# A transformer block in fp32 accuracy on one core: the last moving tile of each change is loaded and split at another place

## The reference

```
u = _rms(h, g_mlp_pre[l])
f = jnp.square(jax.nn.relu(u @ w_ff1[l])) @ w_ff2[l]
h = h + _rms(f, g_mlp_post[l])
```

## Time and profile before

| | |
|---|---|
| median of 3 runs | 2652.94 us (2649.47 to 2654.08) |
| profiled execution, span | 2651.5 us (its own time isn't given beside the span) |
| PE busy | 2577.2 us, 97% |
| DVE, ACT, POOL busy | 1621.5, 1212.6, 334.6 us |
| TensorE's mean granted clock | 0.990 |

### The profile page before, as it was taken

How to read it: one execution, slowest core, us unless ns; L and a number is a source line. 1 busy time by engine, 2 the same in 40 slices (tenths; PEclk the granted TensorE clock), 3 DMA queues, 4 the chain that set the end, 5 groups by cost and what they waited for, 6 DMA issues and landing times.

```text
span 2651.5 us, 35377 instructions
## 1 busy us (share of the span) xinstructions
PE 2577.2 (97%) x12220; PEld 2118.7 (80%) x12220; DVE 1621.5 (61%) x3488; ACT 1212.6 (46%) x2177; POOL 334.6 (13%) x366
## 2 busy tenths in 40 slices
PE   8999999999998999999999999999999999999998
PEld 8998787666676888877877888878887887878786
DVE  6223304989995766764468777766757465564665
ACT  6112312676774555654445333533335343443554
POOL 2110001222221221220000000000000001111133
PEclk9999999899999999999999999999999999999999
DMA  7323457543533111126667667757655365666787
GB/s 235 124 102 117 120 160 243 137 101 80 126 127 92 29 46 40 29 68 189 187 227 224 214 216 230 225 158 231 195 153 177 107 222 104 164 164 158 184 173 139
DMA packets 331516, 398.85 MB, mean 150 GB/s; under 512 B 23488, under 2 KB 237744, under 8 KB 323024
## 3 DMA queue, kind: packets, MB, share of 16 engines
q1 hardware_dynamic: 313776, 364.68, 44.0%
q0 software_dynamic: 17568, 31.99, 8.4%
HBM read 240.13 MB, written 156.48 MB: 150 GB/s over the span
## 4 chain that ended last, share of the span: by engine, by line
PE 61%; DVE 3%; ACT 2%; DMA 1%; issue 1%; SPq 1%; POOL 0%; DVEq 0%; ACTq 0%; POOLq 0%
PE ff_ps_x L3163 25%; PE ff_ps_m L3163 13%; PE ff_ps_z L3163 6%; PE ml_ps_s L2042 6%; PE ff_ps_m L1602 4%; PE ml_ps_o L2071 4%; PE ml_ps_t L2055 2%; DMA ml_v_raw<-scr_yT 1%; DVE ff_mv_lo_p L3014 1%; DMA ff_pieces<-scr_acc 0%; PE ff_ps_r L2602 0%; PE mo_ps_t L2619 0%; ACT ff_mv_hi_p L2896 0%; SPq L2229 0%; DVE ff_pieces L2332 0%
## 5 line engine op out<-in xcount | busy, mean ns | idle before, releaser
L3163 PE MATMUL ff_ps_x<-ff_mv_hi_p,ff_st_hi_p 128*128 128x512 f32 x764 | 299.0, 391 | 12.0 <-DVE ff_mv_lo_p L3014 11.4
L3163 PE MATMUL ff_ps_x<-ff_mv_hi_p,ff_st_lo_p 128*128 128x512 f32 x764 | 298.6, 391 | 0.0
L3163 PE MATMUL ff_ps_x<-ff_mv_lo_p,ff_st_hi_p 128*128 128x512 f32 x764 | 298.3, 390 | 0.0
L2042 PE MATMUL ml_ps_s<-wide,ml_qs 128*128 128x416 f32 (+14 forms) x880 | 196.5, 357 | 3.2 <-PEq L137 2.7
L3009 DVE TENSOR_TENSOR ff_st_lo_p<-ff_ps_m,ff_st_hi_p 128x512 fp32r<-128x512 f32 x190 | 130.8, 689 | 103.7 <-ACT ff_st_hi_p L2886 103.7
L2853 POOL DMA_DIRECT2D scr_acc<-ff_pieces x64 | 55.4, 872 | 1026.2 <-DVE ff_pieces L3033 947.0
L3163 PEld LDWEIGHTS ff_ps_x<-ff_mv_hi_p,ff_st_hi_p 128*128 128x128 f32 x764 | 144.0, 188 | 44.2 <-issue 13.6
L2903 ACT ACTIVATE ff_u<-ff_ps_x 128x512 f32<-128x512 f32 x128 | 76.6, 599 | 214.4 <-PE ff_ps_x L3163 214.4
L3163 PEld LDWEIGHTS ff_ps_x<-ff_mv_hi_p,ff_st_lo_p 128*128 128x128 f32 x764 | 144.0, 188 | 30.2
L3163 PEld LDWEIGHTS ff_ps_x<-ff_mv_lo_p,ff_st_hi_p 128*128 128x128 f32 x764 | 144.1, 189 | 29.9
L2042 PEld LDWEIGHTS ml_ps_s<-wide,ml_qs 128*128 128x128 f32 x880 | 151.0, 191 | 19.1 <-issue 7.0
(11 more groups left out here) (300 smaller groups left out, 6383.3 us busy)
## 6 DMA issues: line engine op xcount, KB each, us to landing
st_raw<-in_w_ff SPq DMA_DIRECT2D x64, 512.0 KB, 6.2
scr_hid<-ff_pieces SPq DMA_DIRECT2D x128, 256.0 KB, 2.6
st_raw<-scr_hid SPq DMA_DIRECT2D x64, 512.0 KB, 5.1
ring<-in_w_ff SPq DMA_DIRECT2D x28, 1024.0 KB, 7.9
scr_t<-ring SPq DMA_DIRECT2D x24, 1024.0 KB, 6.4
ring<-scr_t SPq DMA_DIRECT2D x21, 1024.0 KB, 8.3
scr_acc<-ff_pieces POOLq DMA_DIRECT2D x64, 256.0 KB, 4.1
ring<-scr_u SPq DMA_DIRECT2D x13, 1024.0 KB, 8.3
```

The lines of the kernel that those rows point to most:

```text
L2042: m = pe.matmul(ps_s[n % NSB][:, 0:w], q, k, start=j == 0, stop=j == len(pairs) - 1)
L3163: m = pe.matmul(bank[:, :], w[kind][:, k], a[kind][:, k], start=start and k == 0 and i == 0, stop=stop and k == KH - 1 and i == 2, skip_gr ...
```

## The change

Three orders are altered, and no instruction is added or taken away. SyncE issues the load of the `p4` tile in front of `load_raw(n+2)` at the first step of a group. ScalarE makes its high half before the split of `p2`, VectorE its low half before the sum `c11` and the split of `p2`.

```diff
             def quarters(n):
-                if starts(n):
-                    load_moving(group_of(n), "p4")
                 if ends(n):
...
                 if n:
                     store("c21", n - 1)
-                if n >= 0 and n + 2 <= LAST:
+                if starts(n):
+                    load_moving(group_of(n), "p4")
+                if n + 2 <= LAST:
                     load_raw(n + 2)
                 quarters(n)
...
             for n in range(PLAIN + 1, LAST + 1):
+                if starts(n):
+                    load_moving(group_of(n), "p4")
                 if n + 2 <= LAST:
                     load_raw(n + 2)
...
# ScalarE
-                then("p2", n)
                 if starts(n):
                     moving("p4", group_of(n))
+                then("p2", n)
...
# VectorE
                     mean(n - 1, 0, 2)
+                if starts(n):
+                    moving("p4", group_of(n))
                 if n:
                     dve.wait_ge(product_done, done("p2", n))
                     add("c11", n, ps_z, s1, c11_made)
                 then("p2", n)
                 hidden("c11", n, c11_made)
-                if starts(n):
-                    moving("p4", group_of(n))
```

## The result

| | median | range, runs |
|---|---|---|
| before | 2652.94 us | 2649.47 to 2654.08, 5 |
| changed | 2636.0 us | 2634.19 to 2637.34, 5 |

The kernel before has two more runs here than in its first table; the median stayed. The medians differ by 16.9 us; 2638.0 us was forecast. The ratio of the runs is 0.9943, 95% interval 0.9931 to 0.9955, which is 15.1 us less (11.9 to 18.3). The span of the profiled execution fell from 2651.5 to 2635.5 us (2636.5 forecast).

The account below looks back on a forecast made before the run. TensorE, busy 97% of the span, was taken to bound the kernel. 15.95 - 5 x 0.2 = 14.95 us off the 2651.5 us span gave 2636.5, plus 1.4 for the median: 2638.0 us, range 2634.5 to 2643.0.

Parts of the forecast that it names:

- the cost of a change: TensorE at five moving-tile changes: 11.4 us of gaps plus 4.55 us of slow products behind them, together 15.95 us.
- ScalarE's and VectorE's splits: Step 16: ScalarE's tile copy begins at 1723.93 instead of 1726.27, VectorE's low half runs 1725.86 to 1728.16.
- The residue: Left at each change on TensorE: 0.1 us lateness plus up to 0.12 us slower first matmuls; 0.2 us taken.
- The load: SyncE issues the p4 tile 1.3 us earlier in step 16; landing 0.7 us before ScalarE comes, at old flight.
- rival B: Tile lands no earlier or VectorE's order costs: ScalarE waits 0.6 us each change, 3.2 us in all; 2641.2 us; chance 0.09.
- rival A: Clock still falls at two changes, steps 40 and 56, though gaps go: 3.46 us stay, 2641.4 us; chance 0.11.
- C: VectorE's 1.8 us of lead were needed each change; TensorE waits for a later low half, 9 us back, 2647 us; chance 0.04.
- D: Tile lands late, holding up both splits: at five changes 15.4 us more than before, 2668 us; chance 0.03.
- E: Reorder moves nothing because ScalarE doesn't come to the p4 tile earlier: 2653 us; chance 0.05.

Follow-up runs that it names:

- splits alone: Changed kernel with SyncE's old order, so the p4 load stays behind the raw rows: 2636.18 us against 2649.96 us before, ratio 0.9945.
- one product earlier: Changed kernel with ScalarE's p4 split also ahead of the p7 copy, VectorE's ahead of sum c22: 2633.31 us against 2649.96 us before, ratio 0.9932.
- VectorE's order kept: Changed kernel with VectorE's low half of p4 back behind sum c11 and the split of p2: 2642.37 us against 2649.96 us before, ratio 0.9968.
- load alone: Kernel before with only SyncE's p4 load moved ahead of the raw rows, both splits in old order: 2651.41 us against 2649.96 us, ratio 0.9999.
- ScalarE's order kept: Changed kernel with ScalarE's split of p4 back behind that of p2: 2650.51 us against 2651.91 us before, ratio 0.9999.
- double copy: Kernel before with ScalarE's copy of the p4 tile made twice at the five changes: 2663.83 us against 2651.91 us, ratio 1.0047.
- late tile: Changed kernel with the p4 load behind the raw rows and a wait for p3's next low half: 2665.51 us against 2651.91 us before, ratio 1.0054.

## Why the prediction was right

- **What bounds the kernel, and the cost of a change** (15.95 us): right. The clean length of the feed-forward fell by 14.9 us, for 14.95 us forecast.
- **ScalarE's and VectorE's splits:** right to 0.1 us in each place. The two experiments that move only one of them show that both were needed.
- **The residue** (0.2 us taken, 0.1 to 0.24 bounded): measured 0.21 to 0.24, at the upper end. The product behind was to take about 2.8 us; counted from the end of `p1` it takes 2.93 to 2.96. It goes to zero once the low half is ready earlier, so it was the 0.1 us of lateness and what a restart costs besides.
- **The load:** right in kind, too cautious in size, and of little weight. The flight with nothing large ahead was 5.2 to 7.2 us instead of the 7.6 to 9.1 us used. The margins at steps 32 and 56 on which rival B rested, worked out as 0.3 and 0.2 us, were 3.1 and 2.3 us, and with the old order of SyncE only 0.8 us would have been lost.
- **The falls of the clock** (rival A): they belong to the gaps. The products behind the gaps, read from the chain of waits of ten profiles:

| gap on TensorE | kernels | changes | with a fall of the clock | slow product of 2.72 us takes |
|---|---|---|---|---|
| none or up to 0.4 us | changed, splits alone, one product earlier | 15 | 0 | 2.72 to 3.00 |
| 1.1 to 1.7 us | VectorE's order kept | 5 | 0 | 2.96 to 3.00 |
| 2.3 us | before (twice), load alone, ScalarE's order kept | 20 | 8 | 4.2 to 4.6 |
| 4.1 us | double copy | 5 | 5 | 4.5 to 5.5 |
| 3.8 to 5.5 us | late tile | 5 | 5 | 4.3 to 5.5 |

  What the Trainium skill says (TensorE: Matmul & The Clock Gate, section "Why this matters for your kernels"), that long gaps between bursts cost the clock, holds here; what would follow from its figure, that gaps of this length are safe, doesn't: at 2.3 us 8 of 20 had a fall. The measurement decides, and the two falls were rightly put into the sum. Away from the gaps there are none: in stretches of 6 us from 1418 to 2600 us the granted clock of the changed kernel is 1.00 throughout, and so it is with VectorE's order kept and with both splits one product earlier. The price of the two falls, 3.46 us, is a little too high, since the 1.85 us of step 56 hold the 0.28 us of a restart at full clock: 3.2 us is left, and with VectorE's order kept 3.3 us came back. The sum of 15.95 us doesn't change by it, only rival A's time.
- **The time.** 2 us below the point. The feed-forward explains none of it, since it gained 14.9 us for 14.95. The rest is within what executions of one kernel differ by: the five runs of before lie within 4.6 us, those of the changed kernel within 3.2 us, and the profiles enter the feed-forward anywhere within 6.1 us. So it is partly luck that the medians came within 2 us; the length of the feed-forward is what bears the sum out.
- **Rivals C, D and E:** C's cover held. In the changed kernel VectorE, behind the late sum, stands idle again for 0.89 us from about 1732.6 us and for 2.03 us from about 1734.2, so not all of its lead was used up; how much later it could run isn't shown. D's mechanism is real and cost 16.8 us in the profiled execution, but needs this tile to land more than 3 us later than it did in the changed kernel. E is excluded by ScalarE's timeline.

## What to carry to other kernels

Where an engine works through an order written by hand, look at what an instruction waits for *by its place*: a long tile copy whose own data were ready stood behind a short one that waited for the last product, and 2.3 us of TensorE's time a change hung on that alone. Move the whole chain (load, high half, low half) in front of the wait; one link alone brings nothing or half. Price a gap on TensorE with the matmuls behind it, too: here 11.4 us of gaps cost another 3.3 us in clock, and gaps about half as long none in the one execution profiled.

## What the runs showed of the hardware beyond that

- Behind gaps of 2.3 us the granted clock falls at some and not at others: two of five in each of four profiles, at steps 40 and 56, 48 and 56, and twice 40 and 48, never at 16 or 32, with the product 1.5 to 1.9 us longer. Behind 4.1 us it fell at all five, with the product up to 2.7 us longer. What chooses among equal gaps stays open.
- A load of 1 MB took 5.2 to 5.6 us from issue to landing in steps 16, 32 and 40 of the changed kernel, and 6.7 to 8.0 us before with another 1 MB issued just ahead. In steps 48 and 56 it took 7.0 to 7.2 us and 7.5 to 9.1 us. GpSimd's accumulating DMAs run beside it there, but whether they are the cause stays open: in the late-tile kernel they ran beside it in steps 40, 48 and 56, and it took 7.4, 5.7 and 5.8 us.
- A gap costs more than its own length in the product behind, at full clock, too: behind every gap of 0.2 to 2.3 us without a fall the product took 2.96 to 3.01 us instead of 2.72, 0.24 to 0.29 us more.
